# Both products of a doubling level side by side, and nine pieces of projection per turn where there were fourteen

## The reference

```python
def rwkv7_step(state, inp):
    r, w, k, v, a, bb = inp
    sa = jnp.einsum('dbhvk,dbhk->dbhv', state, a)
    state = state * w[..., None, :] + sa[..., :, None] * bb[..., None, :] + v[..., :, None] * k[..., None, :]
    return state, jnp.einsum('dbhvk,dbhk->dbhv', state, r)
...
    z = h @ w_in[l]
    za, zb, zc = jnp.split(z, [NA_IN_COLS, NA_IN_COLS + RW_IN_COLS], axis=-1)
    ya = neighbourhood_attention(qa, ka, va, na_rpb[l])
    yb = rwkv7_mixer(zb, ...)
    yc = retention_mixer(qc, kc, vc, gc)
```

## Time and profile before

| | |
|---|---|
| median of 3 runs | 1312.7 us (1312.68 to 1313.5) |
| the profiled execution | 1312.83 us, of which the span from first to last instruction is 1311.0 us |
| granted clock of TensorE, mean | 0.999 |
| PE busy | 1288.6 us, 98% of the span |
| DVE, ACT, POOL busy | 837.9, 640.2, 325.1 us |
| the six turns | about 130 to 376 us of the span |

### The profile page before, as it was taken

The page is one execution under the profiler, slowest core; times in us unless marked ns, Lnnn a source line. Parts: engine busy times, 40 slices in busy tenths (PEclk is TensorE's granted clock), DMA queues, the critical chain, the costliest instruction groups (busy, mean ns, idle before and its releaser), DMA issues.

```text
span 1311.0 us, 24363 instructions
## 1 busy us (share of the span) xinstructions
PE 1288.6 (98%) x9996; PEld 1105.8 (84%) x9996; DVE 837.9 (64%) x1161; ACT 640.2 (49%) x978; POOL 325.1 (25%) x266
## 2 busy tenths in 40 slices
PE   9999999999999999999999999999999999999997
PEld 8888888778888898788888888888888888888886
DVE  7778888887877977556555555555555555555564
ACT  7565565556433446456444444444444444444453
POOL 0223333233315220001555555554410000000000
PEclk9999999999999999999999999999999999999999
DMA  9666333333475445855766666666666665556672
GB/s 308 186 181 190 97 84 98 98 99 85 124 159 165 113 130 180 298 163 157 219 189 191 192 187 187 191 192 186 188 191 194 192 196 195 194 192 194 194 231 93
DMA packets 267518, 226.23 MB, mean 173 GB/s; under 512 B 15184, under 2 KB 240592, under 8 KB 266768
## 3 DMA queue, kind: packets, MB, share of 16 engines
q1 hardware_dynamic: 267024, 223.44, 56.8%
q0 software_dynamic: 240, 1.18, 0.3%
q10 hardware_dynamic: 144, 0.07, 0.0%
HBM read 222.56 MB, written 2.10 MB: 171 GB/s over the span
## 4 chain that ended last, share of the span: by engine, by line
PE 67%; DVE 4%; issue 1%; ACT 1%; DMA 1%; DVEq 0%; ACTq 0%
PE psum L2422 31%; PE psum L1970 18%; PE psum L1981 9%; PE psum L1954 2%; PE psum L1960 2%; PE psum L1955 2%; DVE w_lo L944 1%; DMA raw<-in_w_out 1%; ACT w_hi L1536 0%; PE psum L2399 0%; PE psum L2368 0%; PE psum L2479 0%; DVE arena L1442 0%; PE psum L2310 0%; PE psum L2390 0%
## 5 line engine op out<-in xcount | busy, mean ns | idle before, releaser
L944 DVE TENSOR_TENSOR w_lo<-raw,w_hi 128x1024 fp32r<-128x1024 f32 x394 | 499.2, 1268 | 372.2 <-ACT w_hi L1536 368.4
L1536 ACT ACTIVATE w_hi<-raw 128x1024 fp32r<-128x1024 f32 x394 | 418.2, 1065 | 452.0 <-PE psum L2422 185.4
L2422 PE MATMUL psum<-w_hi,act_both 128*128 128x512 f32 x1216 | 327.8, 390 | 1.9 <-DVE w_lo L944 1.0
L1970 PE MATMUL psum<-act_both,w_hi 128*128 128x512 f32 x1296 | 315.4, 392 | 0.0
L1970 PEld LDWEIGHTS psum<-act_both,w_hi 128*128 128x128 f32 x1296 | 237.0, 188 | 45.2 <-issue 0.2
L2422 PEld LDWEIGHTS psum<-w_hi,act_both 128*128 128x128 f32 x1216 | 227.9, 188 | 50.4 <-issue 1.7
L2422 PE MATMUL psum<-w_lo,act_both 128*128 128x512 f32 x608 | 187.5, 389 | 0.0
L1981 PEld LDWEIGHTS psum<-act_both,w_lo 128*128 128x128 f32 x1296 | 169.4, 191 | 7.7
L1981 PE MATMUL psum<-act_both,w_lo 128*128 128x256 f32 x1296 | 173.2, 283 | 0.0
L2422 PEld LDWEIGHTS psum<-w_lo,act_both 128*128 128x128 f32 x608 | 114.1, 188 | 23.8
L883 POOL TENSOR_TENSOR arena<-arena 128x512 f32<-128x512 f32 x32 | 42.3, 1323 | 287.8 <-DVE arena L1475 287.8
(11 more groups left out here) (249 smaller groups left out, 1250.8 us busy)
## 6 DMA issues: line engine op xcount, KB each, us to landing
raw<-in_w_up SPq DMA_DIRECT2D x128, 512.0 KB, 4.0
raw<-in_w_down SPq DMA_DIRECT2D x128, 512.0 KB, 4.6
raw<-in_w_in SPq DMA_DIRECT2D x114, 512.0 KB, 4.1
raw<-in_w_out SPq DMA_DIRECT2D x32, 512.0 KB, 4.8
arena<-in_x_t SPq DMA_DIRECT2D x4, 512.0 KB, 7.5
arena<-in_na_rpb SPq DMA_DIRECT2D x16, 128.0 KB, 4.9
arena<-in_x SPq DMA_DIRECT2D x1, 2048.0 KB, 10.8
out_x<-arena SPq DMA_DIRECT2D x3, 512.0 KB, 2.7
```

The source lines that it names most:

```text
L944: dve.tensor_tensor(by_half(h, low(h)), by_pair(h, raw[:, place[h] % RAW]), by_half(h, high(h)).bitcast(F32), ALU.subtract).then_inc(s["lo ...
L1536: act.activation(by_half(h, high(h)), by_pair(h, raw[:, place[h] % RAW]), ACT.Copy).then_inc(s["hi_half"], 1)
L1970: last = pe.matmul(bank[b], w_hi[:, h % SPLIT, at:at + P], act_both[:, kt].rearrange("p a t -> p (a t)"), start=kt == 0, stop=stop and kt ...
L2422: last = pe.matmul(bank[4 * t + 2 * j + b], lhs[:, tokens], w[:, b * 512:(b + 1) * 512], start=start, stop=stop)
```

## The change

The first gap of each level is taken away. In a level PE now issues P, the first chunk step, Q, the second chunk step, and only then a gap; the other engines follow in the same order, and the feed pieces that stood in `between` now stand behind this one gap. A turn has 4 + 5 = 9 gaps. The same 352 depths are spread over them, so that a gap has mostly 6 or 7 depths where it had mostly 4. The gaps behind levels 0 to 4 are now, in depths: 6, 7, 6, 7, 6 in turn 0; 7, 6, 7, 6, 7 in turns 1 and 4; 6, 8, 6, 6, 8 in turn 2; 6, 6, 6, 8, 6 in turn 3; 6, 7, 6, 7, 7 in turn 5. Before, by `DONE`, the two gaps of level 1 of turn 4 have 5 and 4 depths.

```diff
-TURN_GAPS, TAIL_GAPS = KEY_GAPS + 2 * len(LEVELS), 3 * NC
+TURN_GAPS, TAIL_GAPS = KEY_GAPS + len(LEVELS), 3 * NC
...
 # POOL
             def level(t, p, n, steps, between, behind):
-                run(steps[:1])
+                run(steps)
                 gap()
                 run(between)
-                run(steps[1:])
-                gap()
                 run(behind)
...
 # DVE
                 take_p(0)
                 take_p(1)
                 run(steps[:1])
-                gap()
-                run(between)
                 take_q(0)
                 take_q(1)
                 run(steps[1:])
                 turn_q(0)
                 turn_q(1)
                 gap()
+                run(between)
                 run(behind)
...
 # ACT
                 run(steps[:1])
-                gap()
                 if n == len(LEVELS) - 1:
                     take_inverse(0)
                     take_inverse(1)
-                    run(steps[1:])
-                    run(between)
-                else:
-                    run(between)
-                    run(steps[1:])
+                run(steps[1:])
                 gap()
+                run(between)
                 run(behind)
...
 # PE
                 make_p()
                 run(steps[:1])
-                gap()
-                run(between)
                 make_q()
                 run(steps[1:])
                 gap()
+                run(between)
                 run(behind)
```

More of the change, by code:

```diff
@@ L507, in gap_of_turn @@
         def gap_of_turn(t, n):
-            return DENSE_GAPS + t * TURN_GAPS + KEY_GAPS + 2 * n
+            return DENSE_GAPS + t * TURN_GAPS + KEY_GAPS + n
         def gap_of_mix(i):
@@ L546, in due @@
             return next(g for g in range(len(DONE)) if DONE[g] >= min(depth, DEPTHS))
-        assert due(16 * (RW_T + 32) + DRAIN_LAG) > gap_of_turn(RW_CT - 1, -2)
+        assert due(16 * (RW_T + 32) + DRAIN_LAG) > gap_of_turn(RW_CT - 1, -KEY_GAPS)
         assert due(16 * (RW_T + 30) + DRAIN_LAG) > gap_of_turn(RW_CT - 2, 2)
```

## The result

The changed kernel takes 1349.5 us (median of 4 runs, 1347.19 to 1351.88) against 1312.7: a ratio of 1.0275, with a 95% interval of 1.0262 to 1.0287. It is 36.8 us slower. The sign was forecast, the size was not: 1328.0 was, with a range up to 1342.

The account below looks back on a forecast made before the run. PE bounds the stage, DVE close behind. 12.1 + 4.1 + 5.7 + 2.0 - 6.3 - 3.5 = +14.1, plus 0.3 for each of four turns, gives +15.3 on 1312.83: 1328.0 us, range 1315 to 1342.

Parts of the forecast that it names:

- P to Q, 12.1 us: In every level PE waits for P's masks, as Q can start only 1.24 us after P's start: 12.1 us lost.
- the rival of the splits: High and low weight halves share gaps more often, so DVE waits for ACT ten more times: 7 us, 1335; chance 0.09.
- Sums in front of level 1, 4.1 us: Running sums, now ahead of level 1's take_p on DVE, delay it in turns 0, 2 and 3: 4.1 us lost.
- ACT's chain in front of u, 5.7 us: In level 1 of turns 1 to 4, u waits for ACT's table load, exponentials and copy behind the sums: 5.7 us.
- more than 1 us in each of turns 1 to 4: Sign in the changed profile: u in level 1 waits for ACT by this much, right behind the exponentials.
- the drain behind a load: Rival: 1.38 us of drain on each ACT table load makes four waits 5.5 us longer together, about 1333.5; chance 0.03.
- Keys in front of the last `take_p`, 2.0 us: In level 3 a weight half and the keys delay DVE's last take_p by 0.5 us in about four turns: 2.0 us.
- the key section gives nothing by itself: No cost there except next-turn masks coming later behind the second direction's feed: 0.3 us for each of four turns.
- The clock: Rival: nine waits in levels 1 and 4 each bring a piece at 1.2 GHz, 19 us in all, 1347; chance 0.05.
- The gain, 6.3 + 3.5 us: Thirty fewer pieces over six turns save 0.21 us each, 6.3; half of PE's idle 6.9 us goes, 3.5.
- The low end of its own range, 1319: Forecast's best case: sums at 1.13 us, all of PE's idle time gone, no cost for keys before the last take_p.
- to cancel the loss: Sign of a wrong prediction: entering and leaving a piece costs much more than 0.21 us; 0.6 us would cancel the loss.

Follow-up runs that it names:

- e3_sums_between: Changed kernel with the feed's running sums put back on DVE between take_p with the first step and take_q: 1341.6 us, ratio 1.0213.
- e4b_splits_early: Changed kernel with the turns' weight splits due up to one depth before the end of the piece starting at their gap: 1337.2 us, ratio 1.0178.
- e1_two_gaps: Changed kernel with two gaps per level kept, both behind Q, so fourteen gaps per turn: 1327.1 us, ratio 1.0105 to the kernel before.
- the run with long fillers: Changed kernel with 16, 13, 13 and 7 unread 128 by 128 matmuls in front of Q in levels 1 and 4: 1352.3 us, ratio 1.0295.

## Why the prediction was wrong

**P to Q, 12.1 us: right in sum.** The step was that Q can start 1.24 us after P. It starts after 1.34 wherever DVE is free (P at 311.46, Q at 312.80), with waits of 0.15 behind u and 0.4 behind g, 0.67 in turn 0 and 0.75 in level 4. These bare waits add up to 12.0 us. That this is so near 12.1 is in part luck: behind the state step PE waits nothing (forecast 0.13), in level 3 it waits 0.39 (forecast 0.13), and level 4 and turn 0 come a little cheaper. The waits of L2203 and L2206 together are 20.5 us against 12.1 + 4.1 + 2.0 = 18.2 forecast for hand-over, sums and keys. What is beyond that is mostly one wait of 1.47 in level 0 of turn 1, for a mask behind a weight half that had itself waited for ACT (the rival of the splits, in a level), and 0.6 more in level 3 of turn 0.

**Sums in front of level 1, 4.1 us: the size was right, the remedy was not.** Beyond the bare 0.4 (0.67 in turn 0), the waits of level 1 are 1.4, 0, 1.3, 1.3 and 0 us in turns 0 to 4. The forecast had 1.5, 0, 1.3, 1.3, 0. But with the sums back between the masks 3.2 of the 4.0 us stay (`e3_sums_between`), so the waits cannot be put down to where the sums stand alone; DVE has the same work between the masks of level 0 and those of level 1 either way.

**ACT's chain in front of u, 5.7 us: wrong.** u waits for it at most 0.24 us (turns 2 and 3), where more than 1 us in each of turns 1 to 4 was named as a sign. "From the load's start to the next free moment it takes 2.23 us" counted the table load behind the sums. The load runs ahead of the wait (299.01, the sums end at 301.2), and only the exponentials remain, 302.19 - 301.26 = 0.93 us, which the mask and Q nearly cover. In the earlier trace rows the load had followed the sums only because ACT came late. So the drain behind a load that the Trainium skill gives (ScalarE: Activation LUTs, What ACT_TABLE_LOAD costs) does not show in this chain either: the exponential starts 0.97 us after the load's end, sooner than 1.38, and 0.04 after its data; in turn 4 it starts 0.02 us behind the load (349.18). The measurement decides.

**Keys in front of the last `take_p`, 2.0 us: about right.** The last level's waits are 6.9 us, 2.4 above six times 0.75.

**The step that failed: what stands in the key section.** The sum says "the key section gives nothing by itself", with 1.2 us for masks behind the second direction's feed, and the rival "the splits come just in time" got 0.09 and 7 us, "against it: in a level ACT starts its split long before DVE has transposed". I had looked for it in the levels. It came in the key section, where the pieces grew as well and masks, evictions and weight halves stand behind each other on DVE. There PE waits 13.6 us: 6.4 for weight halves, 3.3 for evictions, and 3.9 for the masks, in two waits and not in four of 0.3. Another 2.7 us for weight halves lie in the levels. Splits due earlier took 11.5 us of these waits away and gave 12.3 us back (`e4b_splits_early`); fourteen gaps with their depths in the levels gave back 22.4 (`e1_two_gaps`).

**The clock, which the sum had at nothing: the rival had 0.05 and came to pass in part.** There were five falls, not nine, and 10.3 us of full speed missing, not 19. The earlier trace rows bore out one wait of 1.3 us without a fall; the changed kernel has twelve of 1.3 us or more in the turns. The falls are not bound to single waits: it fell after 1.47 us (turn 1) and 1.71 (turn 3), and not after 2.25, 2.22 and 2.16 (turns 2, 4 and 5). The Trainium skill (TensorE: Matmul & The Clock Gate, HAM oscillation) warns that waits between bursts of matmuls bring the lower clock. This trace agrees that the falls come behind waits, with the granted clock at 0.90 over turn 3; the page's example has longer waits, for transfers, and which wait brings a fall no run here shows.

**The gain, 6.3 + 3.5 us.** PE's busy time grew by 6.2 us while 10.3 of speed was missing, in stretches where PE was busy almost throughout. That leaves some 4 us of busy time saved, near the 6.3 forecast; that it is the switches is argued, not measured by itself. That half of the idle 6.9 us would vanish cannot be seen under 30 us of new idle time.

**Two sums of the prediction do not come out.** The low end of its own range, 1319, is about 1322 by the terms it names. And a piece would have to cost about 0.7 us, not 0.6, to cancel the loss: 30 * 0.7 = 21 against 15.3 + 6.3. Neither changes what failed.

Summed up: PE waits 20.5 us at the hand-over and 16.2 elsewhere, 37 us idle where it was idle for 6.9; with 6.2 us more busy time (10 for the clock, less about 4) that makes the 36.4 us of the turns. The forecast had 18 and 5.7 of waits in the levels, 1.2 in the key section and nothing for the clock.

## What to carry to other kernels

Where engines execute their lists in order, a long filler is not only cover for PE but a calendar for the others. What falls due at each piece is issued in a lump. As I read these runs, fewer and longer pieces make every dependent engine's work lumpier, and the lump lands in front of something that PE waits for. Before merging pieces to save a switch (0.21 us by the prediction's rows), set against it the bare hand-over that it uncovers (1.34 us from product to product through PSUM, mask and back) and the queue of the masking engine at that point, in every section whose pieces change, not only in those whose order does. A single level tried alone in the old kernel (10 us for level 4, where the rows gave 4) would have shown in one run that the forecast was too low.

## What was not expected of the hardware

A table load on ACT does not wait for the data of the activation behind it: it ran at 299.01, the activation waited until 301.26. A 128 by 128 fp32 matmul held PE 0.24 us, twice my estimate, with two records in the trace for each. Half speed lasted through nearly a whole piece of 6 depths (3.85 us instead of 2.27) and followed waits of 1.3 to 2.1 us in turns 0 to 3, but not waits of 2.2 us in turns 2, 4 and 5; in the run with long fillers it did follow waits of 2.2 us at these same places.
